# The first modulation's bias in the accumulators and its last weights in halves; the last expert outside the counted loop, with halved activations and last transfers

## The reference, cut to what matters

```python
shift1, scale1, gate1, shift2, scale2, gate2 = silu(c) @ w_mod + b_mod      # per stream, 6 x 1024
hn   = rmsnorm(x, norm_mix_w) * (1 + scale1) + shift1
proj = hn @ w_in                                  # 512 pool | 1920 RWKV | 2048 merge columns
x    = x + gate1 * (sig(mergeA) * pool_branch + sig(mergeB) * rwkv_branch) @ w_o
hn2  = rmsnorm(x, norm_ffn_w) * (1 + scale2) + shift2
for e in range(32):                               # top 4 of 32 experts per token
    gu  = hn2 @ w_gu[e] + b_gu[e]                 # 1024 -> 2048
    act = min(gate, 7) * sigmoid(1.702 * min(gate, 7)) * (clip(up, -7, 7) + 1)
    out = out + combine[:, e] * (act @ w_down[e] + b_down[e])
y    = rmsnorm(x + gate2 * out, norm_final_w)
```

## Time and profile before

| what | value |
|---|---|
| median of the runs | 1228.42 us |
| profiled execution | 1228.45 us, span 1226.7 us |
| PE busy | 1182.4 us (96%) |
| DVE, ACT, POOL busy | 383.6, 195.0, 35.3 us |
| read from HBM | 462.37 MB, 378 GB/s over the span |
| instruction fetches (q8) | 32, 0.52 MB |

### The profile page before, as it was taken

One profiled execution on the slowest core, in us unless ns is written; L12 is line 12 of the kernel. 1 busy time (PEld: TensorE's weight loads), 2 busy tenths in 40 slices (PEclk: granted clock), 3 DMA queues, 4 the chain that ended last, 5 costly groups with the idle time before them and its releaser, 6 DMA issues.

```text
span 1226.7 us, 17192 instructions
## 1 busy us (share of the span) xinstructions
PE 1182.4 (96%) x6971; PEld 554.6 (45%) x6971; DVE 383.6 (31%) x854; ACT 195.0 (16%) x361; POOL 35.3 (3%) x78
## 2 busy tenths in 40 slices
PE   5999999999999999999999999899999999999997
PEld 2777889988333333333333333333333333333333
DVE  3577894363412111112221221311112221121112
ACT  2340223201311111111121111111111111111102
POOL 3000110110000000000000000000000000000000
PEclk9999999999999999999999999989999999999999
DMA  9999312499999999999999999999999999999995
GB/s 366 341 329 311 106 59 87 151 392 410 388 431 427 428 427 428 428 430 430 428 426 427 427 409 427 427 427 428 431 428 427 428 428 427 428 430 429 428 427 232
DMA packets 67752, 464.34 MB, mean 379 GB/s; under 512 B 8151, under 2 KB 31342, under 8 KB 41726
## 3 DMA queue, kind: packets, MB, share of 16 engines
q1 hardware_dynamic: 64560, 458.11, 90.7%
q0 software_dynamic: 1504, 4.75, 1.1%
q10 hardware_dynamic: 1646, 0.86, 0.2%
HBM read 462.37 MB, written 1.34 MB: 378 GB/s over the span
## 4 chain that ended last, share of the span: by engine, by line
PE 74%; DMA 22%; DVE 2%; issue 1%; ACT 1%; SPq 0%; DVEq 0%; ACTq 0%
PE bank L1391 28%; DMA ring<-in_expert_w_gu 20%; PE bank L1461 12%; PE sums L722 5%; PE sums L743 4%; PE sums L1489 3%; PE sums L1195 2%; PE sums L1268 2%; PE bank L1303 2%; DMA ring<-in_w_mod 2%; PE bank L1340 2%; PE sums L665 1%; PE bank L1430 1%; PE sums L867 1%; PE bank L1331 1%
## 5 line engine op out<-in xcount | busy, mean ns | idle before, releaser
L1391 PE MATMUL bank<-ring,gate 128*64 128x512 f32 x1992 | 441.9, 599 | 16.7 <-DMA ring<-in_expert_w_gu 16.7
L1391 PEld LDWEIGHTS bank<-ring,gate 128*64 128x64 f32 x1992 | 140.0, 138 | 314.5 <-issue 284.0
L1461 PE MATMUL bank<-ring,gate 128*64 128x512 f32 x960 | 212.6, 595 | 3.3 <-DVE gate L2336 1.3
L2326 DVE TENSOR_SCALAR gate<-bank 128x512 f32<-128x512 f32 x32 | 22.1, 692 | 382.8 <-PE bank L1391 382.8
L1461 PEld LDWEIGHTS bank<-ring,gate 128*64 128x64 f32 x960 | 68.4, 137 | 126.8 <-issue 126.4
L1834 ACT ACTIVATE corr<-gate 128x512 f32<-128x512 f32 x32 | 20.1, 630 | 658.6 <-DVE gate L2326 658.6
L2352 DVE TENSOR_TENSOR corr<-bank,spare 128x512 f32<-128x512 f32 x31 | 21.4, 691 | 221.7 <-PE bank L1461 221.7
L1489 PE MATMUL sums<-corr,kk 64*128 64x512 f32 x248 | 61.6, 615 | 0.0
L1303 PE MATMUL bank<-qr,vt 128*64 128x512 f32 x256 | 60.4, 592 | 0.0
L722 PE MATMUL sums<-hnT,ring 128*128 128x256 f32 x256 | 56.4, 380 | 0.0
L743 PE MATMUL sums<-hnT,ring 128*128 128x256 f32 x240 | 54.9, 383 | 0.7 <-ACT hnT L1563 0.7
(11 more groups left out here) (427 smaller groups left out, 993.6 us busy)
## 6 DMA issues: line engine op xcount, KB each, us to landing
ring<-in_expert_w_gu SPq DMA_DIRECT2D x123, 2048.0 KB, 19.1
ring<-in_expert_w_down SPq DMA_DIRECT2D x62, 2048.0 KB, 19.1
ring<-in_w_mod SPq DMA_DIRECT2D x24, 1024.0 KB, 11.1
ring<-in_w_in SPq DMA_DIRECT2D x17, 1024.0 KB, 10.1
ring<-in_w_o SPq DMA_DIRECT2D x3, 1024.0 KB, 8.6
ring<-in_expert_w_gu SPq DMA_DIRECT2D x3, 1024.0 KB, 14.2
more<-in_expert_w_down SPq DMA_DIRECT2D x2, 1024.0 KB, 7.2
ring<-in_w_pool_out SPq DMA_DIRECT2D x2, 1024.0 KB, 4.9
```

The lines of the kernel that those rows point to most:

```text
L1391: last = mm(b[h * SLOTS:(h + 1) * SLOTS, :], xg[:, 2 * (u % 2) + i, u // 2, :], w(u, i, j, h), start=False, stop=(u == GU_UNITS - 1 and i ...
L1461: last = mm(DN[h * SLOTS:(h + 1) * SLOTS, :], actT[:, i, u, :], w(GU_UNITS + u, i // 2, i % 2, h), start=(u == 0 and i == 0), stop=(u == D ...
```

## The change

What it does at the front:

- The last `A` chunk is fetched as two of 1024 columns: shift1's (slot 7), then scale1's (slot 10). PE makes group 0's last four matmuls, then waits for ACT's copy and makes group 0's transposes, and only then group 1's. Group 0's copy to SBUF and `moda[:, 0]` are ACT's, group 1's copy is DVE's, and its transposes go to bank 0.
- The bias of both groups is added by eight matmuls with 8 rows (columns of the identity times `brow`, b_mod as eight rows of 256, a new small transfer on ACT's queue) ahead of the chunks, with `start=True`. DVE's three operations after the transposes become two, which read the bank.
- Column tiles 12 to 14 of w_in come as two chunks of 384 columns by 512 rows (slots 0 and 1), where they came as 256 and 128 columns by 1024 rows. Each of these three projections takes four k-tiles of each.
- Transposed tiles k of xn lie in banks by k's parity; ACT writes the even tiles of hnT, DVE the odd.

What it does at the end:

- The counted loop holds item 30 and the extra items, and expert 31 always comes last, outside it, written as its own code (`last_down`, `last_expert`). The list of extra items counts from 31 downwards for this.
- Expert 31's units 3 and 5 are fetched as two transfers each, with a semaphore each. Unit 3's matmuls are made for its first half (gate, up), then for its second.
- Its activation is made in two halves (`pairs`: columns 4c + 0, 1 and 4c + 2, 3) on DVE and ACT; transposes go to bank 6, two for each half, with ACT copying; the second half's transposes stand inside the down matmuls. The combine weights are transposed after unit 0. The second half of the down product goes to bank 4.
- It makes no gather and no bias for a next expert.

```diff
-            out.append(("w_mod", 0, 2 * D, i, slot, ("moda_mm", i + 1)))
+            out.append(("w_mod", 0, 2 * D, i, slot, ("moda_mm", i + 1)) if i < KT - 1 else
+                       ("w_mod", D * (i - KT + 1), D, KT - 1, slot, ("moda_mm", i + 1)))
         elif kind == "B":
             out.append(("w_mod", D * (2 + i // MC), D, 2 * (i % MC), slot, ("modb_mm", i + 1)))
         elif kind == "R":
-            n = 256 if i < RTILES // 2 else P
-            done = max(POS[t] for t in (2 * i, 2 * i + 1) if t < RTILES) + 1
-            out.append(("w_in", POOLW + 256 * i, n, 0, slot, ("proj_done", done)))
+            if i < LOW // 2:
+                done = max(POS[t] for t in (2 * i, 2 * i + 1)) + 1
+                out.append(("w_in", POOLW + 256 * i, 256, 0, slot, ("proj_done", done)))
+            else:
+                out.append(("w_in", POOLW + P * LOW, LOWW, 4 * (i - LOW // 2), slot, ("proj_done", RTILES - LOW)))
         elif kind == "P":
             out.append(("w_in", 256 * i, 256, 0, slot, ("pu_mm", i + 1)))
...
-        n_items = sp.value_load(item[0:1, ITEMS:ITEMS + 1], min_val=NE, max_val=NE + EXTRA)
-        with sp.Fori(NE - 1, n_items) as it:
+        at_last = sp.value_load(item[0:1, ITEMS:ITEMS + 1], min_val=LAST, max_val=LAST + EXTRA)
+        with sp.Fori(LAST - 1, at_last) as it:
             expert(it, sp.value_load(item[0:1, bass.ds(it, 1)], min_val=0, max_val=NE - 1))
+        before_last = sp.value_load(item[0:1, ITEMS + 1:ITEMS + 2], min_val=LAST - 1, max_val=LAST - 1 + EXTRA)
+        for u in range(NU):
+            sp.wait_ge(S("chunk_used"), before_last * NU + (u + 1))
+            if u in IN_HALVES:
+                for i in range(2):
+                    sp.dma_start(ring[:, 2 * u + i, :], unit_src(LAST, u)[:, CW * i:CW * (i + 1)]).then_inc(S(f"slot{2 * u + i}_full"), 16)
+            else:
+                expert_unit(LAST, u)
 
...
+        for g in range(2):
+            for j in range(MG):
+                mm(banks[MODA_BANK[g]][32 * j:32 * (j + 1), 0:TT], ident[0:2 * MG, MG * g + j:MG * g + j + 1].to_broadcast([2 * MG, 32]), brow,
+                   start=True, stop=False)
+
         pe.wait_ge(S("cpad_ready"), 1)
-        for k in range(KT):
+
+        def first_mod(k, g, w):
+
+            for j in range(MG):
+                last = mm(banks[MODA_BANK[g]][32 * j:32 * (j + 1), 0:TT], cpad[:, k, :], w[:, 0, j * MW:(j + 1) * MW],
+                          start=False, stop=(k == KT - 1))
+            return last
+
+        for k in range(KT - 1):
             arrived(pe, AT["A", k])
             w = ring_in(AT["A", k])
-            for g in range(2):
-                for j in range(MG):
-                    last = mm(banks[MODA_BANK[g]][32 * j:32 * (j + 1), 0:TT], cpad[:, k, :], w[:, 0, g * D + j * MW:g * D + (j + 1) * MW],
-                              start=(k == 0), stop=(k == KT - 1))
-            last.then_inc(S("moda_mm"), 1)
+            first_mod(k, 0, w[:, :, 0:D])
+            first_mod(k, 1, w[:, :, D:2 * D]).then_inc(S("moda_mm"), 1)
             if k == 5:
                 pe.wait_ge(S("rows_b_in"), 160)
...
         for g in range(2):
-            pe.wait_ge(S("mrow_ready"), g + 1)
-            mod_turn(mrow_a[:, g, :], banks[6][:, g * MW:(g + 1) * MW], "modat_mm")
+            arrived(pe, AT["A", KT - 1 + g])
+            first_mod(KT - 1, g, ring_in(AT["A", KT - 1 + g])).then_inc(S("moda_mm"), 1)
+            if g == 0:
+                pe.wait_ge(S("mrow_ready"), 1)
+                mod_turn(mrow_a[:, 0, :], banks[6][:, 0:MW], "modat_mm")
+        pe.wait_ge(S("rows_read"), 2)
+        mod_turn(mrow_a[:, 1, :], banks[0][:, MW:2 * MW], "modat_mm")
...
             last.then_inc(S("merge_mm"), 1)
 
-        mm(banks[5][:, :], ones[:], mqr[:].rearrange("p d k t -> p (d k t)"), start=True, stop=True)
+        mm(banks[5][:, 0:TT], ones[:], mqr[:, 0, :, :].rearrange("p k t -> p (k t)"), start=True, stop=True)
+
+        def proj_half(n, i):
+
+            c = AT["R", LOW // 2 + i]
+            arrived(pe, c)
+            w = ring_in(c)
+            for k in range(4 * i, 4 * i + 4):
+                if n == 0:
+                    pe.wait_ge(S(("hna_ready", "hnd_ready")[k % 2]), k // 2 + 1)
+                last = mm(banks[n % 2][:, 0:TT], w[:, k % 4, n * P:(n + 1) * P], hnT[:, k, :], start=(k == 0), stop=(k == KT - 1))
+            if i == 1:
+                last.then_inc(S("proj_done"), 1)
 
         def proj(n):
 
             ct = ORDER[n]
             c = AT["R", ct // 2]
-            if n == 0:
-                pe.wait_ge(S("prb_ready"), 1)
+            if n >= 2:
+                pe.wait_ge(S("raw_copied"), n - 1)
+            if ct >= LOW:
+                proj_half(n, 0)
+                proj_half(n, 1)
+                return
             arrived(pe, c)
             w = ring_in(c)
-            if n >= 2:
-                pe.wait_ge(S("raw_copied"), n - 1)
-            o = (ct % 2) * P if ct < RTILES - 1 else 0
-            for i in range(KT):
-
-                k = (i % 2) * 4 + i // 2
-                if n == 0:
-                    pe.wait_ge(S(("hna_ready", "hnd_ready")[i % 2]), i // 2 + 1)
-                last = mm(banks[n % 2][:, 0:TT], w[:, k, o:o + P], hnT[:, k, :], start=(i == 0), stop=(i == KT - 1))
+            o = (ct % 2) * P
+            for k in range(KT):
+                last = mm(banks[n % 2][:, 0:TT], w[:, k, o:o + P], hnT[:, k, :], start=(k == 0), stop=(k == KT - 1))
             last.then_inc(S("proj_done"), 1)
 
         def decay_mm():
...
+        def last_down(it, skipped):
+
+            def act_turn(b):
+
+                pe.wait_ge(S("act_ready"), it + (b + 1))
+                for i in (2 * b, 2 * b + 1):
+                    last = tr(banks[6][:, i * P:(i + 1) * P], act_[:, i::4], ident[:])
+                last.then_inc(S("actT_done"), 1)
+
+            pe.wait_ge(S("pwt_ready"), it + 1)
+            act_turn(0)
+            pe.wait_ge(S("actT_ready"), it + 1)
+            for u in range(DN_UNITS):
+                unit_in(it, GU_UNITS + u, skipped)
+                for c, i in ([(c, i) for i in range(4) for c in range(2)] if u == 0 else [(c, i) for b in range(2) for c in range(2) for i in (2 * b, 2 * b + 1)]):
+                    if u == 0 and (c, i) == (0, 1):
+                        act_turn(1)
+                    if u == 0 and (c, i) == (0, 2):
+                        pe.wait_ge(S("actT_ready"), it + 2)
+                    if u and (c, i) == (0, 2):
+                        second_half_in(NU - 1)
+                    for h in range(2):
+                        last = mm((DN, G)[c][h * SLOTS:(h + 1) * SLOTS, 0:256], actT[:, i, u, :],
+                                  from_ring(GU_UNITS + u, i // 2, i % 2, h)[:, 256 * c:256 * (c + 1)],
+                                  start=(u == 0 and i == 0), stop=(u == DN_UNITS - 1 and i == 3))
+                    if u and c == 0 and i == 3:
+                        last.then_inc(S("dn_half"), 1)
+                last.then_inc(S("chunk_used"), 1)
+            for c in range(2):
+                cs = slice(256 * c, 256 * c + 256)
+                for s in range(NS):
+                    pe.wait_ge(S("ysb_ready"), it * NS + (2 * c + s + 1))
+                    for h in range(2):
+                        r = slice(h * SLOTS, (h + 1) * SLOTS)
+                        last = mm(banks[2 * s + h][:, cs], pwt[r, s, :], ysb[s][r, cs], start=False, stop=True, skip_group_check=True)
+                    if c:
+                        last.then_inc(S(("scattered_ctx", "scattered_lat")[s]), 1)
 
         def expert(it, skipped, outside=(), half=None, late=False, end=False):
...
+                    up_part(u, L, 1, w, (0,))
+                    second_half_in(u)
+                    up_part(u, G, 0, w, (1,)).then_inc(S("g_mm"), 1)
+                    up_part(u, L, 1, w, (1,)).then_inc(S("chunk_used"), 1)
+                    break
                 last = up_part(u, G, 0, w)
                 if u < at_once:
                     up_part(u, L, 1, w).then_inc(S("chunk_used"), 1)
+                if end and u == 0:
+                    pe.wait_ge(S("pw_ready"), it + 1)
+                    for s in range(NS):
+                        tail = tr(banks[6][:, s * T:(s + 1) * T], pw[:, s, :], ident[:])
+                    tail.then_inc(S("pwt_done"), 1)
+            if end:
+                last_down(it, skipped)
+                return
...
+        act.wait_ge(S("pwt_done"), at_last + 1)
+        af(pwt.rearrange("p s t -> p (s t)"), banks[6][:, 0:TT], ACT.Copy).then_inc(S("pwt_ready"), 1)
+        for b in range(2):
+            act.wait_ge(S("g_ready"), at_last + (b + 1))
+            af(pairs(sgb, b), pairs(gsb, b), ACT.Sigmoid, scale=ALPHA).then_inc(S("sg_ready"), 1)
+        for b in range(2):
+            act.wait_ge(S("actT_done"), at_last + (b + 1))
```

(39 more changed lines are left out.)

185 lines of the change are left out of this document (88 added, 97 removed).

## The result

The kernel after takes 1231.41 us (median of 13 runs), the kernel before beside it 1228.82: the ratio is 1.0022 with a 95% interval of 1.0015 to 1.0030. It is slower, by 2.6 us in the medians, and outside the range of the prediction, 1225.0 to 1228.7. The profiled execution of after took 1229.8 (span 1228.0 against 1226.7).

What follows compares the result with a forecast made beforehand. PE's serial chain was taken to bound the front, and the last gate/up landing plus activation the tail. Front 0.0 and tail 1.7 us (1.75 rounded down) took 1228.4 to 1226.7 us, range 1225.0 to 1228.7.

Steps and rivals of the forecast that it cites:

- The sum: Whole kernel: front 0.0 plus tail 1.75 us won, rounded to 1.7 for register waits, giving 1226.7 us.
- Bias matmuls, 1.07: Front: eight bias matmuls add 1.07 us to PE's work, timed like the eight of the last chunk.
- The bias's transfer, 0.2 (0 to 0.34): Front: one more small transfer before the first transpose delays PE's chain by 0.2 us, possibly 0 to 0.34.
- First half of chunk 7: Front: matmuls on the first half of the last modulation chunk start at 27.0 us, PE rather than the transfer being late.
- First projection at 31.15: Front: the chain behind the modulation lets the first projection start at 31.15 us, against 31.20 before.
- w_in's second half at 33.0: Front: second merged w_in chunk lands at 33.0 us (31.0 to 34.0), when PE is half through the first projection.
- Front net: Front: gains and costs cancel to 0.0 us, with ends of -0.25 and +1.0.
- rival B: Tail: new code layout puts instruction fetches on engines with slack, tail starts 1.2 us sooner, 1225.5 us; chance 0.27.
- The tail up to U: Last expert's gate/up matmuls: PE skips a 1.25 us wait; up sum ready at 1206.1 us, was 1207.4, landings unchanged.
- The down phase, 7.13 + 0.37: Tail: down matmuls take 7.13 us as before, plus 0.37 for the second pair's transposes inside them.
- D: Front and tail: split transfers' halves land 2.4 us late, front +2.4, tail loses 0.3, giving 1231.1 us; chance 0.09.
- C: Front and tail: halves bring little, DVE crowded, front's second half lands near 34; 0.5 us net, 1227.9; chance 0.11.

Runs made afterwards that it cites:

- e3: Kernel after plus 128 waits on an already full semaphore at PE's head, shifting only its code; PE's stall in y(1) was 2.43 us.
- e4: Kernel after plus 22 idle matmuls behind the last up matmul; they took 4.75 us; turns to last down matmul 8.7 us against 10.2 in after.
- e10: Kernel after plus 8 idle matmuls in the last activation; the three first projections came 1.16 us later than in before.
- e1: Kernel before with the front's edits alone, last expert unchanged; its front cost 2.68 us, and the 0.85 us stall was there.
- e12: e10 with w_in's last tiles in their old shape; of 11 runs five at 1227.3 to 1228.4 us, six at 1229.3 to 1230.9.
- e11: e10 without the bias matmuls and the bias's transfer, bias added by VectorE as before; runs 1227.1 to 1228.5 us.
- e9: Kernel before with the last expert's edits alone plus 8 idle matmuls in the last activation; 1227.08 us against 1228.77, ratio 0.9987.
- e14: e10 with the same 16 bias matmuls moved behind the third chunk's matmuls; eleven runs from 1227.1 to 1229.3 us.
- e7: Kernel before plus 54 idle matmuls of 60 columns at PE's head; the first matmul behind the three first projections came 15.7 us later.
- e5: Kernel after plus 45 idle matmuls of 72 columns at PE's head; last gate or up matmul to end 20.83 us.
- e6: e5 plus 8 idle matmuls in the last activation; last gate or up matmul to end 19.27 us.

## Why the prediction was wrong

The sum was 1.75 us down and the profiled execution went 1.26 up. Of the 3.0 between them the front is 0.7, the fetch 0.9, and the stretch behind U 1.8; up to U it went 0.4 better than forecast.

**Bias matmuls, 1.07.** They took 1.33 in after, half of it before the clock's rise at 15.4, and 0.99 (e3, e4, e10) or 1.86 (e1, e12) elsewhere. Right in size for a settled clock; but I took the neighbours' time from a stretch at 2.4 GHz and did not see that this place lies where the clock rises, at 15.1 in before and 14.2 to 19.9 in the others.

**The bias's transfer, 0.2 (0 to 0.34).** The first transpose came 0.42 later, at 9.36; over the traces without matmuls at the head it comes at 9.3 to 9.7 with the transfer and at 8.8 to 9.3 without. It pushes the end only because PE had no gap left; that was foreseen.

**First half of chunk 7 at 27.0.** 27.16: right. **First projection at 31.15.** 31.58: 0.16 from the start, 0.27 from small steps that were each up to 0.08 longer than the rows they were taken from.

**w_in's second half at 33.0.** 33.58 with a wait of 0.44, inside the stated 31.0 to 34.0. My choice was mis-sized by 0.6 to 1.1 over the traces. Front net predicted 0.0, with +1.0 as an end; measured +0.68, in repeats of this front +1.05 to +1.16.

**What was not in the sum: PE's own instruction fetch.** I put a price on the new code layout only through fetches that delay a DMA engine (rival B), and none on PE running dry. That is 0.93 us and the first step that failed; e3 and e11 show it, where the stall went with the layout.

**The tail up to U.** Forecast: 1.3 sooner with the landings unchanged. Measured: 1.48 by the stretch from unit 2's landing to U, and Y to U 1.70 shorter. PE's waits are gone as said, and this part of the mechanism was right. The sign set for rival B, unit 2 at other than 6.2 us behind unit 1, did come, with 4.9, but not its gain: the last 16 KB fetches before U came at 1166.0 and 1189.5 (1193.6 before), and the landings spread behind them too, only earlier, so unit 2 landed 0.22 sooner behind Y and not 1.2. Over all traces the old tail has 963.8 to 964.7 from Y to U and the new one 962.1 to 963.5.

**The down phase, 7.13 + 0.37.** It took 9.16, with the clock kept 7.71. This is the second step that failed, and the larger. The first down matmul came 5.1 us behind unit 3's landing, just as forecast, and the scatter 14.2 behind it instead of 12.6, so the loss lies in this phase alone. I wrote that PE has "only fillers" in the activation and let them go at no cost, without asking what else they did. They kept PE's clock. The Trainium skill (TensorE: Matmul & The Clock Gate, Part 1) says that an idle PE is gated to 1.2 GHz; the window row with 0.52 agrees, and e9's 1.00 with the 8 calls shows the cure.

**The rivals.** D's time, 1231.1, is next to the measured median of 1231.41, and that is luck: its mechanism, halves that land late by 2.4 us each, did not happen. PE waited 0.4 to 0.8 at the front, and at the tail unit 3's halves landed 2.5 us apart, 1202.57 and 1205.05, which is their 1.05 MB at 423 GB/s. The fixed part that the Trainium skill gives a DMA (DMA: Bandwidth & Descriptors, section "Anatomy of one DMA", measured there on GpSimd's path, where these are issued by SP) does not show there, for transfers that are queued behind others. C had the halves bringing 0.5 and w_in's second half landing near 34; the landing was so in e3, e4, e10 and e14, but up to U the tail's halves did bring 1.5, and C lacked the two costs that decided.

**What stays open.** The profiled executions differ by 1.26, the medians by 2.6. Five of after's 13 runs lie at 1233.3 to 1233.8, the rest at 1228.4 to 1231.4. A slow start such as e1's, +2.0, would explain the five, but none of them was traced, and there is a rival: their mean granted clock was 0.990 or 0.991, as in three of the other eight, where the five remaining runs had 0.993, with a median of 1230.6. The long runs of e1 and e12 do not differ from their short ones in it. All of e10's runs had 0.992 to 0.994. Its median is 2.7 us below that of after, where the idle calls account for 1.5, but only 1.9 below that of after's five runs at 0.993. Where the clock was lost in the long runs, and whether that made them long, is not shown: the profiled execution had 0.990 too and took 1229.8.

## What to carry to other kernels

Work that "only fills" PE's waits may be holding its clock: before it is dropped, look at the granted clock behind the gap, and if the gap stays, put back as much idle work as fits, priced from a row of the same form and per record. An edit changes the code layout for all that follows; when a trace shows PE idle on "issue" in the middle of equal matmuls, suspect the fetch, move the code to test it, and put its price down to the layout and not to the edit. Splitting a transfer so that its first half comes sooner makes everything behind wait for a second landing; count that landing, and not only the first. A gap between two landings tells the rate only while their spread stays the same: compare each landing with a mark of the kernel, and not with its neighbour.

## What the runs showed of the hardware

- PE stood 0.85 us (after, e1, e4, e10, e12, e14) and 2.43 us (e3) for a block of its own instructions. The block could be used 1.2 to 1.5 us behind the end of its packet, and within 0.4 us of the same time wherever in the code its boundary lay.
- A 16 KB instruction fetch among the weights' transfers widened the spread of a unit's 16 landing events for all later units: 2.3 to 3.6 us in before, 1.8 to 2.6 in after.
- Two halves of 1.05 MB queued one behind the other landed 2.5 us apart (after), with no extra time for the second.
- The idle matmuls at the head took 0.216 us a record, and 19.5 us of them without a gap (23.3 in e7) did not raise the clock; it rose at 27.1, when PE had gone on to the transposes and come to the bias matmuls (33.0 in e7, among the modulation's).
- The granted clock fell at 1210.0, after an idle time of 1.9 us and in a second one of 0.5, and cost 1.5 us (e5 against e6); with 1.7 us of idle matmuls in the first of them it did not fall.
- From 44 to 195 us every trace follows that of before within 0.02 us but for a constant: what is lost at the front by then is carried on whole.
